# Two transformer blocks on one core: the last norm on VectorE with a store per chunk, half of each boundary's sum ahead of the last square, and weight blocks of the heads split in four parts

## The chip, the core and the metric

The kernel runs on one NeuronCore of a Trainium2 chip. The metric is the device time of one execution in microseconds. In the text PE is TensorE, DVE is VectorE, ACT is ScalarE, POOL is GpSimd and SP is SyncE, which here only issues transfers. L661 is line 661 of the kernel before.

## What is computed

The reference chains two models, each of two layers, over 512 tokens of width 1024, all in fp32. The first has attention with 12 heads in each layer (8 of kind A, over latents, and 4 of kind B, differential), gates, and a convolutional feed-forward part, over 512 tokens and, in its first layer, 256 context tokens beside them. The second has a pooling and gating mixer in layer 0, a sparse attention and retention mixer in layer 1, and a SwiGLU part after each. The parts of it that the change touches are the norms between stages and the end:

```python
def rms_norm(x, g):
    xf = x.astype(jnp.float32)
    y = xf * lax.rsqrt(jnp.mean(xf * xf, axis=-1, keepdims=True) + EPS)
    return (y * g.astype(jnp.float32)).astype(x.dtype)

    for layer in range(DEPTH):          # the second model
        h = rms_norm_2(x, ln_mix_pre[layer])
        m = even_mixer(h, ...) if layer % 2 == 0 else odd_mixer(h, ...)
        x = x + rms_norm_2(m, ln_mix_post[layer])
        h = rms_norm_2(x, ln_ffn_pre[layer])
        x = x + rms_norm_2(swiglu(h, ...), ln_ffn_post[layer])
    return x
```

## The kernel before

Activations lie transposed in SBUF: 8 chunks (DC) of 128 channels by 512 tokens. Every fp32 product is made of three matmuls of split operands (high by high, high by low, low by high; mm3, L661 to L663, and the same for several outputs at once, mm3_side, L676 to L678). Each engine has a program of its own in a fixed order written out by hand; they meet at semaphores only, so an engine that waits holds up all that stands behind it in its program.

**Weights.** The weights are cut into blocks of mostly 128 x 2048 words, in the order of split_order(). SP loads a block into one of two raw slots. ACT copies it with rounding into the high half of one of two split slots (act_prepare, L621), which must be free: the product that used it two blocks ago must have ended. DVE subtracts to get the low half (dve_prepare, L632), after which PE may use the block (pe_block) and SP may load the next into the raw slot. One block is one ACT instruction and one DVE instruction, put by hand between other work.

**Heads.** head_items() makes one list of steps for a layer's 12 heads, and PE, ACT and DVE each walk it, each doing its own share of a step: projections of queries and keys (a_q, a_k, v_b, b_qk, b_rope), early gates, scores (PE L1264, maximum on DVE L1587, exp on ACT L1410, division on DVE "weigh" L1492 to L1502), "turn" (PE transposes L1296, ACT L1420, DVE L1595) and "values". A turn is one chunk of 256 keys of one pair of query tiles; each turn holds at most a few pieces of the next head's projections. 13 blocks are prepared in each layer's list, each at the point where the product that held its slot has just ended.

**Boundaries.** Between stages a norm needs the sum over all 1024 channels of the squares. ACT squares a chunk (L692, chunk 0 in L705), POOL adds chunks 1 to 6 to chunk 0 (L715), and PE sums over the channels with a matrix of ones: pe_square_summed, L718, one fp32 matmul for POOL's sum (L722) and one for the square of chunk 7 (L723), each recorded as two. ACT then makes the logarithm (L728) and the root (L733). After the out projection (act_out_linear) a chunk is first copied out of PSUM (act_evict, L2174) and then squared. DVE applies the norm, adds to x and makes the low half of the next input chunk by chunk (dve_post_gained: L2124, L2128, L2088), while ACT makes the high halves (act_gained_highs, L2073). At the end of act_out_linear, and of act_glu and dve_glu in layer 0, one block is prepared between the last square and the logarithm, on ACT and on DVE.

**End.** After the last feed-forward part DVE multiplies the eight chunks (dve_post_norm, L2117), POOL adds each to x (pool_post_norm, L2137), and one transfer of 2048 KB stores all (L3536).

## Time and profile before

| | us |
|---|---|
| median of 3 runs | 3604.68 (3600.24 to 3604.97) |
| the profiled execution | 3599.33, of it the span 3597.3 |
| PE busy | 3355.3 (93%) |
| DVE busy | 1954.5 (54%) |
| ACT busy | 1394.8 (39%) |
| POOL busy | 334.0 (9%) |
| DMA | 321.93 MB, mean 89 GB/s |

The span runs from the first to the last instruction of the core. PE's matmuls overlap each other and their ends are modelled, so its busy share says where it works, not how well. The trace lists every instruction with its start and length, and, in brackets, how long its engine had been idle and which instruction ended that. A mean granted clock of 1.0 is TensorE's full 2.4 GHz.

### The profile page before, as it was taken

What the parts mean: (1) busy time and instruction counts of PE and PEld (TensorE: products, weight loads), DVE (VectorE), ACT (ScalarE), POOL (GpSimd) and SP (SyncE); (2) the same over time, 40 slices, a digit from 0 to 9 for tenths busy, and PEclk for the clock granted to TensorE, in tenths of its full rate; (3) what the DMA queues carried; (4) which work ended last, traced back from release to release, by engine and by line L of the source; (5) the groups of instructions that cost most, each with busy time, mean ns of one, the idle gap of its engine ahead of it and who ended that gap; (6) DMA issues with size and microseconds to landing.
All of it is one profiled execution on the core that took longest, in us unless ns stands there. A gap on an engine that the chain in (4) does not pass through costs nothing.

```text
span 3597.3 us, 41937 instructions
## 1 busy us (share of the span) xinstructions
PE 3355.3 (93%) x17348; PEld 2804.3 (78%) x17348; DVE 1954.5 (54%) x2794; ACT 1394.8 (39%) x2200; POOL 334.0 (9%) x277
## 2 busy tenths in 40 slices
PE   8889898999999997898899999899999989989997
PEld 5778777888888886787777888787888767768886
DVE  5674555677736635756535635455444566345243
ACT  4563443234313324644434323344222356243221
POOL 0010000221101110000011101121000210210002
PEclk9999999999999999999899999999999999999999
DMA  5001114343323422011133332322222310122322
GB/s 224 32 26 50 50 39 163 133 145 123 113 83 127 137 76 70 19 63 46 59 132 123 128 106 87 101 94 85 90 104 88 108 37 35 59 70 87 107 87 72
DMA packets 74495, 321.93 MB, mean 89 GB/s; under 512 B 8897, under 2 KB 17857, under 8 KB 52289
## 3 DMA queue, kind: packets, MB, share of 16 engines
q1 hardware_dynamic: 74304, 319.25, 25.9%
q8 instruction: 137, 2.24, 0.3%
q14 instruction: 54, 0.43, 0.0%
HBM read 303.49 MB, written 15.73 MB: 89 GB/s over the span
## 4 chain that ended last, share of the span: by engine, by line
PE 49%; DVE 5%; ACT 3%; issue 1%; POOL 0%; DMA 0%; POOLq 0%; DVEq 0%; ACTq 0%; SPq 0%
PE psum L661 14%; PE psum L663 14%; PE psum L662 14%; PE psum L1264 1%; ACT split_weights L621 1%; DVE split_weights L632 1%; PE psum L1296 1%; ACT arena L1410 0%; PE psum L2560 0%; DVE arena L2124 0%; PE psum L676 0%; DVE arena L1587 0%; PE psum L2975 0%; PE psum L677 0%; PE psum L678 0%
## 5 line engine op out<-in xcount | busy, mean ns | idle before, releaser
L661 PE MATMUL psum<-split_inputs,split_weights 128*128 128x512 f32 (+1 forms) x2864 | 1055.0, 368 | 19.5 <-DVE split_weights L632 14.0
L662 PE MATMUL psum<-split_inputs,split_weights 128*128 128x512 f32 (+1 forms) x2864 | 1046.2, 365 | 0.0
L663 PE MATMUL psum<-split_inputs,split_weights 128*128 128x512 f32 (+1 forms) x2864 | 1045.4, 365 | 0.0
L632 DVE TENSOR_TENSOR split_weights<-arena,split_weights 128x2048 fp32r<-128x2048 f32 (+3 forms) x246 | 506.2, 2058 | 483.5 <-ACT split_weights L621 483.1
L661 PEld LDWEIGHTS psum<-split_inputs,split_weights 128*128 128x128 f32 x2864 | 544.1, 190 | 113.0 <-DVE split_weights L632 17.2
L662 PEld LDWEIGHTS psum<-split_inputs,split_weights 128*128 128x128 f32 x2864 | 543.9, 190 | 87.9 <-issue 2.8
L663 PEld LDWEIGHTS psum<-split_inputs,split_weights 128*128 128x128 f32 x2864 | 543.0, 190 | 87.9
L621 ACT ACTIVATE split_weights<-arena 128x2048 fp32r<-128x2048 f32 (+3 forms) x246 | 414.0, 1683 | 162.2 <-PE psum L663 162.1
L661 PE MATMUL psum<-split_hidden,split_weights 128*128 128x512 f32 (+1 forms) x880 | 324.1, 368 | 2.4 <-DVE split_weights L632 2.4
L662 PE MATMUL psum<-split_hidden,split_weights 128*128 128x512 f32 (+1 forms) x880 | 323.9, 368 | 0.0
L663 PE MATMUL psum<-split_hidden,split_weights 128*128 128x512 f32 (+1 forms) x880 | 323.7, 368 | 0.0
L715 POOL TENSOR_TENSOR arena<-arena 128x512 f32<-128x512 f32 x84 | 107.0, 1278 | 1025.2 <-ACT arena L692 1023.0
L661 PEld LDWEIGHTS psum<-split_hidden,split_weights 128*128 128x128 f32 x880 | 165.9, 189 | 31.1 <-DVE split_weights L632 3.5
L663 PEld LDWEIGHTS psum<-split_hidden,split_weights 128*128 128x128 f32 x880 | 165.9, 189 | 27.7
L662 PEld LDWEIGHTS psum<-split_hidden,split_weights 128*128 128x128 f32 x880 | 165.9, 189 | 27.2
L1264 PE MATMUL psum<-split_high 128*128 128x512 f32 (+3 forms) x864 | 154.1, 362 | 35.0 <-ACT arena L1410 26.9
L1640 DVE CUSTOM_DVE_ANT_0 arena<-arena 128x1024 f32<-128x1024 f32 x128 | 164.8, 1287 | 27.8 <-DMA arena<-w_ada_dram 24.3
L1587 DVE TENSOR_REDUCE arena<-psum 128x1 f32<-128x768 f32 (+1 forms) x160 | 132.3, 845 | 86.4 <-PE psum L1264 85.6
L692 ACT ACTIVATE arena<-arena 128x512 f32<-128x512 f32 (+1 forms) x131 | 75.7, 588 | 260.5 <-DVE arena L1969 98.1
L1264 PEld LDWEIGHTS psum<-split_high 128*128 128x128 f32 (+1 forms) x864 | 121.0, 199 | 68.4 <-ACT arena L1410 35.5
L1410 ACT ACTIVATE arena<-psum,arena 128x768 f32<-128x768 f32 (+1 forms) x160 | 129.6, 813 | 51.0 <-DVE arena L1587 50.5
L1979 POOL TENSOR_TENSOR arena<-arena 128x512 f32<-128x512 f32 x66 | 72.9, 1105 | 726.0 <-DVE arena L1946 726.0
(353 smaller groups left out, 4784.6 us busy)
## 6 DMA issues: line engine op xcount, KB each, us to landing
arena<-w_up_dram SPq DMA_DIRECT2D x44, 1024.0 KB, 5.9
arena<-ffn_up_dram SPq DMA_DIRECT2D x44, 1024.0 KB, 4.8
arena<-w_ada_dram SPq DMA_DIRECT2D x80, 512.0 KB, 3.8
arena<-w_in_dram SPq DMA_DIRECT2D x32, 1024.0 KB, 4.9
arena<-w_down_dram SPq DMA_DIRECT2D x32, 704.0 KB, 4.2
arena<-ffn_down_dram SPq DMA_DIRECT2D x32, 704.0 KB, 4.1
arena<-od_w_in_dram SPq DMA_DIRECT2D x13, 1024.0 KB, 4.8
arena<-w_ada_dram SPq DMA_DIRECT2D x8, 1024.0 KB, 12.6
```

Of the source, the lines that this page charges most:

```text
L621: act.e.activation(ws[:, i % N_SLOTS, 0, 0:nk * w], raw_view(key), ACT.Copy).then_inc(*w_hi(*key))
L632: dve.e.tensor_tensor(ws[:, i, 1, 0:nk * w], raw_view(key), ws[:, i, 0, 0:nk * w].bitcast(F32), ALU.subtract).then_inc(*w_lo(*key))
L661: pe.e.matmul(dst, a[0], b[0], start=i == 0, stop=False)
L662: pe.e.matmul(dst, a[0], b[1], start=False, stop=False)
L663: ins = pe.e.matmul(dst, a[1], b[0], start=False, stop=i == n - 1)
L692: act.e.activation(row, view, ACT.Square, **more).then_inc(*squared(site, s, c))
L715: pool.e.tensor_tensor(acc, acc, rows.at(site, s, c)[:, 0:w], ALU.add).then_inc(*rows.back((site, s, c), pooled, site, s, c))
L1264: return pe.e.matmul(psum[:, at_bank + x:at_bank + y], a, b, start=i == 0, stop=i == 2)
L1410: act.e.activation(row[:, 0:p["keys"]], psum[:, b:b + p["keys"]], ACT.Exp, bias=st[:, sub:sub + 1], accum_out=st[:, 2 + sub:3 + sub]).then ...
L1587: dve.e.tensor_reduce(st[:, sub:sub + 1], psum[:, b:b + p["keys"]], AX.X, ALU.max, negate=True).then_inc(*maxed(l, t, sub))
L1640: dve.e.tensor_tensor_reduce(part.get("junk", rstd_all), ADA[slots[n % len(slots)]], wide[:, s, :], 1.0, 0.0, ALU.mult, ALU.add, mods[al][ ...
L1979: pool.e.tensor_tensor(ya, ya, yb, ALU.mult).then_inc(*added("up", l, half, m, s))
```

## The change

It has five parts.

1. pe_square_summed waits for the last square after the matmul of POOL's sum and not ahead of it.
2. In act_out_linear chunk 7 is squared straight from PSUM and copied out after that.
3. The block that was prepared between the last square and the logarithm moves: ACT makes its high half in two halves behind the high halves of chunks 2 and 4 (act_gained_highs), DVE its low half at the end of dve_post_gained, ahead of the block that was there already. This holds for three boundaries: behind each out projection and behind layer 0's feed-forward part.
4. The last norm and its addition are both on DVE, chunk by chunk one behind the other, and SP stores each chunk of 256 KB when it is done.
5. In the heads each prepare becomes four of a quarter. They queue up in a list, preps; at the end of a turn's pieces at most two are put out, and the rest is put out ahead of a step that takes a new block (v_b, b_qk of queries, the first gate of a chunk). The wait for the slot and the raw block stands ahead of each; PE waits for the last quarter only.

```diff
--- before.py
+++ after.py
@@ -308,6 +308,9 @@
             "ffn": halves(layer, 20, 24, 2) + halves(layer + 1, 0, 8, 2) + halves(layer + 1, 8, 20, 1)}[stage]
 
 
+PARTS = 4
+
+
 def head_items(layer, engine):
 
 
@@ -372,7 +375,7 @@
         out += [("late",) + x for x in step if x[0] in ("a_q", "a_k")]
     out += start
     out += [("weigh", t) for _, t in start]
-    late, weigh, values, ob = [], [], [], {}
+    late, weigh, values, ob, preps = [], [], [], {}, []
 
     def of_values(x, i, c):
 
@@ -405,15 +408,25 @@
             out += scores[0:1]
         weigh = [t for _, t in scores]
         of_norm(x, "ob_root")
-        out += gates[x]
+        if gates[x] and gates[x][0][2:] == (LAT, 0):
+            out += preps
+            preps = []
+        out += [y for y in gates[x] if y[0] != "prepare"]
+        preps += [("prepare", part, PARTS) for y in gates[x] if y[0] == "prepare" for part in range(PARTS)]
         late += [("gate_out",) + y[1:] for y in gates[x] if y[0] == "gate"]
         for step in plan[x]["pieces"]:
-            out += step
+            if step[0][0] == "v_b" or step[0][0] == "b_qk" and step[0][3:] == (0, LAT):
+                out += preps
+                preps = []
+            out += [y for y in step if y[0] != "prepare"]
             late += [("late",) + y for y in step if y[0] in ("a_q", "a_k")]
+            preps += [("prepare", part, PARTS) for y in step if y[0] == "prepare" for part in range(PARTS)]
+        for _ in range(min(len(preps), 2)):
+            out.append(preps.pop(0))
         out += scores[1:]
         of_norm(x, "ob_norm")
         of_norm(x, "ob_square")
-    out += late
+    out += late + preps
     for x, y in enumerate(values, len(slots)):
         of_values(x, *y)
         of_norm(x, "ob_square")
@@ -608,30 +621,44 @@
             _, nk, w = block_shape(*key)
             return raw[raw_slot(key)][:, 0:nk * w]
 
-        def act_prepare():
+        def part_of(part, n):
+
+            return slice(0, n) if part is None else slice(part[0] * n // part[1], (part[0] + 1) * n // part[1])
+
+        def act_prepare(part=None):
+
             if act_next[0] == len(blocks):
                 return
             key = blocks[act_next[0]]
-            act_next[0] += 1
+            last = part is None or part[0] == part[1] - 1
+            act_next[0] += last
             _, nk, w = block_shape(*key)
-            i = block_no[key]
+            i, cols = block_no[key], part_of(part, nk * w)
             if i >= N_SLOTS and book:
                 act.wait_ge(product, *book["ended"][blocks[i - N_SLOTS]])
             act.wait_ge(raw_in[raw_slot(key)], *key)
-            act.e.activation(ws[:, i % N_SLOTS, 0, 0:nk * w], raw_view(key), ACT.Copy).then_inc(*w_hi(*key))
-
-        def dve_prepare():
+            act.e.activation(ws[:, i % N_SLOTS, 0, cols], raw_view(key)[:, cols], ACT.Copy).then_inc(
+                *(w_hi(*key) if last else w_hi(*key, part[0])))
+
+        def dve_prepare(part=None):
+
             if dve_next[0] == len(blocks):
                 return
             key = blocks[dve_next[0]]
-            dve_next[0] += 1
-            use(key)
+            last = part is None or part[0] == part[1] - 1
+            dve_next[0] += last
+            if part is None or part[0] == 0:
+                use(key)
             _, nk, w = block_shape(*key)
-            i = block_no[key] % N_SLOTS
-            dve.wait_ge(w_hi, *key)
-            dve.e.tensor_tensor(ws[:, i, 1, 0:nk * w], raw_view(key), ws[:, i, 0, 0:nk * w].bitcast(F32),
-                                ALU.subtract).then_inc(*w_lo(*key))
-            free(key)
+            i, cols = block_no[key] % N_SLOTS, part_of(part, nk * w)
+            if last:
+                dve.wait_ge(w_hi, *key)
+            else:
+                dve.wait_ge(w_hi, *key, part[0])
+            ins = dve.e.tensor_tensor(ws[:, i, 1, cols], raw_view(key)[:, cols], ws[:, i, 0, cols].bitcast(F32), ALU.subtract)
+            if last:
+                ins.then_inc(*w_lo(*key))
+                free(key)
 
         def pe_block(*key):
             pe.wait_ge(w_lo, *key)
@@ -717,9 +744,9 @@
 
         def pe_square_summed(site, s, n, w, which):
             pe.wait_ge(pooled, site, s, n - 2)
-            pe.wait_ge(squared, site, s, n - 1)
             ps = banks.take(pe, site, s, place=6 + which)
             pe.e.matmul(ps[:, 0:w], ones, rstd[:, which, 0:w], start=True, stop=False)
+            pe.wait_ge(squared, site, s, n - 1)
             pe.e.matmul(ps[:, 0:w], ones, rows.at(site, s, n - 1)[:, 0:w], start=False, stop=True).then_inc(
                 *rows.back((site, s, n - 1), product, "square", site, s, n - 1))
 
@@ -1353,7 +1380,7 @@
             for item in head_items(l, "act"):
                 what, at = item[0], item[1:]
                 if what == "prepare":
-                    act_prepare()
+                    act_prepare(at)
                 elif what == "a_q":
                     n, h, s = at
                     hi = q_half(n, 0)[:, s[0]:s[1]]
@@ -1506,7 +1533,7 @@
             for item in head_items(l, "dve"):
                 what, at = item[0], item[1:]
                 if what == "prepare":
-                    dve_prepare()
+                    dve_prepare(at)
                 elif what == "a_q":
                     n, h, s = at
                     if s == LAT:
@@ -2072,6 +2099,8 @@
                 act.wait_ge(halves_sum, y_site, c)
                 act.e.activation(h2_part(c, *ALL)[0], X2[:, c, :], ACT.Copy, scale=v2(l, gname, c)).then_inc(
                     *h_hi(site, c))
+                if c in (2, 4):
+                    act_prepare((c // 2 - 1, 2))
             for c in range(DC):
                 act_square_summed(site, ALL, c, DC, T2, 1, X2[:, c, :])
 
@@ -2113,9 +2142,14 @@
 
         def dve_post_norm(site, l, gname):
             dve.wait_ge(rooted, site, ALL)
-            for c in range(DC):
-                dve.e.scalar_tensor_tensor(out=MX[:, c, :], in0=MX[:, c, :], scalar=v2(l, gname, c), in1=rstd[:, 0, :],
-                                           op0=ALU.mult, op1=ALU.mult).then_inc(*normed(site, c))
+            for c in range(DC + 1):
+                if c < DC:
+                    dve.e.scalar_tensor_tensor(out=MX[:, c, :], in0=MX[:, c, :], scalar=v2(l, gname, c),
+                                               in1=rstd[:, 0, :], op0=ALU.mult, op1=ALU.mult).then_inc(*normed(site, c))
+                if c:
+                    dve.wait_ge(normed, site, c - 1)
+                    dve.e.tensor_tensor(X2[:, c - 1, :], X2[:, c - 1, :], MX[:, c - 1, :], ALU.add).then_inc(
+                        *conv("final", c - 1))
 
         def dve_post_gained(site, l, gname, then, then_l, then_gname):
             dve.wait_ge(rooted, site, ALL)
@@ -2130,11 +2164,7 @@
                 if c > 1:
                     dve_gained(then, v2(then_l, then_gname, c - 2), c - 2)
             dve_prepare()
-
-        def pool_post_norm(site):
-            for c in range(DC):
-                pool.wait_ge(normed, site, c)
-                pool.e.tensor_tensor(X2[:, c, :], X2[:, c, :], MX[:, c, :], ALU.add).then_inc(*added(site, c))
+            dve_prepare()
 
 
         HS_REST = hs[:, 2 * DC * T2:2 * DC * N_TOK].rearrange("p (s c t) -> p s c t", s=2, c=GC)
@@ -2190,10 +2220,14 @@
             for m in range(DC):
                 if m % 2 == 0:
                     act_prepare()
+                if m == DC - 1:
+                    act.wait_ge(product, name, m)
+                    act_square_summed(site, ALL, m, DC, T2, 0, banks.at(name, m))
+                    act_evict((name, m), MX[:, m, :])
+                    continue
                 act_evict((name, m), MX[:, m, :])
                 act.wait_ge(copied, name, m)
                 act_square_summed(site, ALL, m, DC, T2, 0, MX[:, m, :])
-            act_prepare()
             act_log(site, ALL, DC, T2, 0, D)
             act_root(site, ALL, T2, 0)
 
@@ -2391,8 +2425,6 @@
                 act_prepare()
                 act.wait_ge(conv, "glu_down", l, c)
                 act_square_summed(("ffn", l), ALL, c, DC, T2, 0, MX[:, c, :])
-            if l == 0:
-                act_prepare()
             act_log(("ffn", l), ALL, DC, T2, 0, D)
             act_root(("ffn", l), ALL, T2, 0)
 
@@ -2427,8 +2459,6 @@
                 dve.wait_ge(copied, "glu_down", l, 0, c)
                 dve.e.tensor_tensor(MX[:, c, :], MX[:, c, :], banks.at("glu_down", l, 1, c), ALU.add).then_inc(
                     *banks.back(("glu_down", l, 1, c), conv, "glu_down", l, c))
-            if l == 0:
-                dve_prepare()
 
 
         BIG = 1.5 * 2.0 ** 23
@@ -3318,7 +3348,7 @@
                     dve.e.tensor_tensor(lo, OY[:, h, :], hi.bitcast(F32), ALU.subtract).then_inc(*h_lo("od_y", ALL, h))
 
         def dve_out_linear():
-            for _ in range(DC // 2 + 1):
+            for _ in range(DC // 2):
                 dve_prepare()
 
 
@@ -3526,15 +3556,15 @@
                 if l == 0:
                     for c in range(DC):
                         pool_square_summed("mix_1", ALL, c, DC, T2, 1)
-            pool_post_norm(("ffn", 1))
 
         def sync_program():
             sp_setup()
             for what in errands:
                 sp_errand(*what)
-            sp.wait_ge(added, ("ffn", DEPTH - 1), DC - 1)
-            sp.e.dma_start(out.rearrange("(c p) t -> p c t", p=P), X2).then_inc(*stored())
-            sp.wait_ge(stored)
+            for c in range(DC):
+                sp.wait_ge(conv, "final", c)
+                sp.e.dma_start(out[c * P:(c + 1) * P, :], X2[:, c, :]).then_inc(*stored(c))
+            sp.wait_ge(stored, DC - 1)
 
         block = ctx.enter_context(nc.Block())
```

## Rows read from the trace of the kernel before

**Rows 1.** Page: the header.
```profile
span 3597.3 us, 41937 instructions
```
**Rows 2.** PE's waits over the whole span: us in total, times, longest.
```profile
PE psum L722 <- issue: 5.9, 4, 1.6
...
PE psum L722 <- ACT arena L692: 3.0, 2, 1.6
```
**Rows 3.** Timeline of PE at the end: start, length, line, shape, count, idle.
```profile
3573.72 1.10 PE L722 MATMUL psum<-arena 128*128 128x512 f32 x2 [1.49 <-issue]
3574.66 1.02 PE L723 MATMUL psum<-arena 128*128 128x512 f32 x2
```
**Rows 4.** Timeline of ACT at the boundary behind layer 0's out projection.
```profile
2445.13 0.60 ACT L2174 ACTIVATE arena<-psum 128x512 f32<-128x512 f32 x1 [4.17 <-PE psum L663]
2445.76 0.63 ACT L692 ACTIVATE arena<-arena 128x512 f32<-128x512 f32 x1
...
2448.48 0.69 ACT L728 ACTIVATE arena<-psum,arena 128x512 f32<-128x512 f32 x1 [0.29 <-PE psum L723]
```
**Rows 5.** Timeline of DVE at the same boundary.
```profile
2448.22 2.29 DVE L632 TENSOR_TENSOR split_weights<-arena,split_weights 128x2048 fp32r<-128x2048 f32 x1 [8.58 <-ACT split_weights L621]
2450.43 1.41 DVE L2124 SCALAR_TENSOR_TENSOR arena<-arena 128x512 f32<-128x512 f32 x2
2451.76 0.68 DVE L2128 TENSOR_TENSOR arena<-arena 128x512 f32<-128x512 f32 x1
2452.36 0.75 DVE L2124 SCALAR_TENSOR_TENSOR arena<-arena 128x512 f32<-128x512 f32 x1
...
2464.53 1.63 DVE L2088 SCALAR_TENSOR_TENSOR split_inputs<-arena,split_inputs 128x512 fp32r<-128x512 f32 x2
```
**Rows 6.** Timeline of PE at the same boundary: the next block's first matmul.
```profile
2468.31 0.39 PE L661 MATMUL psum<-split_inputs,split_weights 128*128 128x512 f32 x1
```
**Rows 7.** Timelines of DVE, POOL and SP at the end.
```profile
3577.10 10.40 DVE L2117 SCALAR_TENSOR_TENSOR arena<-arena 128x512 f32<-128x512 f32 x8 [4.14 <-ACT arena L733]
...
3577.93 11.57 POOL L2137 TENSOR_TENSOR arena<-arena 128x512 f32<-128x512 f32 x8 [10.41 <-DVE arena L2117]
...
3589.52 0.39 SPq L3536 DMA_DIRECT2D out_dram<-arena  x1
```
**Rows 8.** Page: a DMA issue, with count, KB each, us to landing.
```profile
g_store<-arena SPq DMA_DIRECT2D x16, 256.0 KB, 2.0
```
**Rows 9.** PE's waits in the heads of layer 0, 116 to 616 us.
```profile
PE psum L1296 <- DVE arena L1494: 11.8, 7, 5.2
...
PE psum L1264 <- DVE split_high L1595: 5.4, 1, 5.4
PE psum L1296 <- DVE arena L1502: 4.3, 2, 4.2
...
PE psum L1243 <- DVE split_high L1595: 3.1, 1, 3.1
```
**Rows 10.** PE's waits in the heads of layer 1, 1416 to 1826 us.
```profile
PE psum L1264 <- ACT arena L1410: 15.0, 6, 3.6
```
**Rows 11.** Timelines of ACT and DVE in layer 1's heads, around one prepared block.
```profile
1736.62 1.91 ACT L621 ACTIVATE split_weights<-arena 128x2048 fp32r<-128x2048 f32 x1
...
1738.56 2.29 DVE L632 TENSOR_TENSOR split_weights<-arena,split_weights 128x2048 fp32r<-128x2048 f32 x1 [1.38 <-ACT split_weights L621]
1740.77 1.82 DVE L1587 TENSOR_REDUCE arena<-psum 128x1 f32<-128x768 f32 x2
```
**Rows 12.** Timeline of PE in layer 1's heads.
```profile
1726.09 0.47 PE L661 MATMUL psum<-split_inputs,split_weights 128*128 128x512 f32 x1 [2.11 <-DVE split_high L1595]
...
1736.23 1.43 PE L1264 MATMUL psum<-split_high 64*128 64x512 f32 x12
...
1742.80 2.68 PE L1264 MATMUL psum<-split_high 64*128 64x512 f32 x12 [3.37 <-ACT arena L1410]
```
**Rows 13.** One stretch of layer 1's heads: busy us of each engine, then PEclk.
```profile
1740.00:1800.00 60.00, 49.58 (x258) 40.38 (x258) 37.01 (x56) 28.13 (x54) 0.00 (x0) 0.86 0.19 62
```

## Prediction, made before the changed kernel was run

> **What bounds the kernel now.** First the page: the span is 3597.3 us [rows 1] and PE is the busiest engine by far, so time can only be won where PE stands still, where it runs at a lower clock, or at the end, where it is done. The second view is the list of PE's waits. It shows three kinds of places. At six boundaries PE waits 1.4 to 1.6 us for the last square and then makes both halves of the sum [rows 2]. In the heads it waits for DVE and ACT, up to 5.4 us at a time [rows 9, 10], and the timeline of the third view shows a prepared block just ahead of the long ones [rows 11, 12]. And behind the last matmul nothing runs beside the chain: sum, root, DVE, POOL, store [rows 3, 7]. Elsewhere PE has its weights in time.
>
> The profiled execution took 3599.33 us, 2.03 beyond its span. I sum against its own time; the median of the runs shown is 5.35 above it, and I take the same gap for the changed kernel.
>
> **1. Half of the sum ahead of the last square.** At the end the first half of the sum starts at 3573.72 after 1.49 us of waiting, the second at 3574.66 [rows 3]. The first half so costs 0.94 us, and it fits in the wait: POOL's sum that it needs is a whole chunk of matmuls older. The second half then starts when the square is there, at 3573.72. That is 0.94 us for each of the six boundaries where PE waits (the 4 and 2 waits of [rows 2]): layer 1's out projection and the double boundary of the first model, two out projections and two feed-forward ends of the second. The other places where the sum is made have no such wait (PE has other matmuls to do), and there I take nothing: the same two matmuls in the same order.
>
> **2. The last square straight from PSUM.** At the out projection of the second model the copy starts at 2445.13, the square at 2445.76, the logarithm, which waits for the second half, at 2448.48 [rows 4]; the second half takes 1.02 [rows 3], so it started at 2447.43. Afterwards the square starts at 2445.13 and is there at about 2445.8; the first half of the sum, 0.94 from the product's end at 2445.1, ends at 2446.05, so now the sum itself is late, and the second half starts then: 1.38 us earlier, part 1 included. The copy, 0.60 us, lies beside the second half. This holds twice.
>
> **3. The block moved off the boundary.** At the end, where no block is in the way, DVE starts 3577.10 - 3574.66 = 2.44 us after the second half of the sum [rows 3, 7]. Here that would be 2449.87, but DVE still has its block till 2450.51 and starts at 2450.43 [rows 5]: the block costs 0.56 us already, and would cost all that parts 1 and 2 win if it stayed. Without it DVE starts at 2446.05 + 2.44 = 2448.49, 1.94 us earlier. Behind layer 0's feed-forward part, which looks the same but for part 2, it is 0.94 + 0.56 = 1.5 us. What is late next: DVE works at three instructions a chunk, two of 0.66 and one of 0.60 from start to start, 1.92 us, and ACT has one high half of about 0.7 in that time; half a block is about 1.0 us of ACT (half of 1.91 and some [rows 11]) and just fits behind chunks 2 and 4. On DVE the block now stands behind the last low half, 2.29 us [rows 5], while PE still has its last chunk to do: from the last low half, ended at 2466.16, to the next block's first matmul at 2468.31 were 2.15 us [rows 5, 6], so PE waits 0.1 to 0.2 us for the block. Queued behind the block on DVE is only the next block, needed much later. Net: 2 x 1.8 + 1.4 + 2 x 0.94 (the two boundaries of the first model) = 6.9 us. Bounds: 5.2 if ACT's halves slip by one chunk, 7.5 if PE waits for nothing.
>
> **4. The end.** DVE and POOL together took from 3577.10 to 3589.50, then came one store; from its issue at 3589.52 to the end of the span are 7.8 us [rows 1, 7]. Eight norms took 10.40 us, 1.30 each, while POOL worked beside them; with POOL at rest the same kind takes 0.66 from start to start and an addition 0.60 [rows 5]. So DVE alone does a chunk in 1.26: first addition 1.33 after the start, the seventh at 8.9, the eighth, which has to wait for its own norm, at about 9.5, ended at 10.2. It starts 0.94 us earlier (part 1), at 3576.16, and ends at 3586.35, 3.1 us ahead of POOL. The last store is 256 KB; such stores took 2.0 us to land [rows 8], and 0.4 us of closing work as before: end at 3588.8, 8.5 us earlier, of which 0.94 is part 1. The stores before it have 1.26 us each, and 2048 KB in 7.8 us says that 256 KB move in under 1 us, so none waits for another. Bounds: 7 (the last lands after 3.5) to 9.
>
> The Trainium skill speaks against this part: "DMA: Bandwidth & Descriptors", section "Measured (HBM→SBUF, 128 partitions, SWDGE, issued from GpSimd)", wants transfers of 1 MiB or more, since small ones pay the fixed cost each time. The sum above has it paid once, behind the last chunk; paid eight times in a row it is the third rival below. By the fit on that page of the Trainium skill (about 2.0 us plus bytes over 436 GB/s, an estimate of 2.6 us for 256 KB) the end would come 0.6 us later than by the row; no row here shows a run of small stores.
>
> **5. Quarters in the heads.** The terms are in one example [rows 11, 12]. ACT starts the block at 1736.62, DVE waits for it, subtracts 2.29 us, and only at 1740.77 takes the maximum of scores whose matmuls had started at 1736.23 and took 1.43. Then comes exp, then PE, which stood still for 3.37 us, and does in 2.68 us 12 matmuls of the kind that took 1.43 before the wait: the granted clock of this stretch is 0.86 [rows 13], so part of it ran at 1.2 GHz instead of 2.4.
> With two quarters DVE waits 0.63 (ACT's time for 512 columns [rows 4]) and subtracts twice, 0.60 from start to start [rows 5]: 1.9 us instead of 4.15, so DVE goes on 2.25 us earlier. Four in a row, where a step takes a new block, hold it for 3.1. All four cost ACT about 2.2 instead of 1.9 and DVE 2.4 instead of 2.2; over 26 blocks that is 5 to 8 us of either, which is lost only where that engine is the late one.
> What it gives, wait by wait:
> - layer 1, three waits of about 3.4 before double scores (most of the 15.0 us in [rows 10]): 2.2 each, 6.7.
> - layer 0: of the 5.4 before L1264, where the rope steps now also come first, 1.8; of the 4.2 before L1296, 1.9; of the 5.2 before L1296 only 0.7, since there DVE is the late engine and gets the other two quarters one turn on; of the 3.1 before L1243 and its twin on the other buffer, 0.9 each, since a block that used to lie in an idle stretch of DVE now lies closer to them [rows 9]. Together 6.2.
> - some nine waits of 1.5 to 2.5 us that follow a block in either layer, about half a microsecond each where ACT or DVE comes out of the block sooner, 5 in all (an estimate from the 2.25 above, a quarter of it each).
> - the clock: behind each of the three large waits up to 1.7 us of slow matmuls; the waits left are about 1.1. I take 3 of 5.
> - against it a new wait. The second two quarters come one turn later, and PE may be there first. I find it at two gates of layer 1. At one, PE's first gate matmul at 1726.09 already waited 2.11 us [rows 12]; the block's last quarter would be ready at about 1725.5, so of these 2.1 only 0.6 go (counted among the small ones). At the gate before it PE would wait about 1.3.
> - and the other two quarters of some 20 blocks hold DVE a second time, 1.2 to 1.9 us, mostly while PE is in 24 or 48 matmuls of a projection (5 to 11 us of cover). If a fifth of them isn't covered, 4 lost.
> 6.7 + 6.2 + 5 + 3 - 1.3 - 4 = 15.6 us, say 16. Bounds: 0 (every second pair is late) to 28 (all clock, nothing lost).
>
> A second rule of the Trainium skill, "VectorE: DVE Perf Modes", section "The TRN2 errata — SBUF-src ops pay a fixed extra latency per instruction", says that each instruction with operands in SBUF pays a fixed latency, so splitting costs. By that fit of the Trainium skill four quarters would take 2.76 us, 0.47 more than one of 2.29; back to back the row has 0.60 from start to start, 2.4 in all. By the Trainium skill's figure the quarters would give 2 or 3 us less.
>
> **Sum.** 6.9 + 8.5 + 16 = 31.4. 3599.33 - 31.4 = 3567.9; with the 5.35 to the median 3573.3, say 3573.
>
> **Rivals.**
> - The gain in the heads fades: the wait only moves a turn, because DVE has as much to do as before. DVE is busy 62% of [rows 13], PE 83%, which speaks against it; that the 5.2 us wait sits in a stretch where DVE is late speaks for it. Then only 15.4 are won: 3589. Chance 0.2.
> - The clock comes back too: the short waits no longer bring TensorE down, and most of the 5 us and those in layer 0 are won, with no new waits: 31.4 + 13 = 44: 3560. Chance 0.15.
> - The stores pay in turn, each 2.0 us [rows 8] behind the one before: from the first addition's end at 3578.2 the last lands at 3594.2 and the span ends at 3594.6, 2.7 instead of 8.5 won: 3579. The rows speak for overlap only by the rate of one large store. Chance 0.07. (The rule of the Trainium skill above would point this way.)
> - Slower than before: the second pair of quarters holds DVE 1.9 us at each of some 20 turns with no cover, and PE's gates wait for the last quarter. 20 x 1.9 = 38 lost, the first pairs win nothing against it, and with 15.4 won it is 22.6 slower: 3627. It decides if DVE has less than 1.9 us idle in those turns. In [rows 13], where parts of three blocks fall, it is idle 23 of 60 us. Chance 0.03.
> - The change doesn't do what it says in part 1: POOL's sum comes as late as the square, and PE waits as before. 6 us fewer, 3579. A chunk of matmuls lies between the two; chance 0.02.
>
> **How the numbers follow.** My case has 0.53: 3573, by itself 3563 to 3583. The range of 8 in 10 takes in the rival without the heads and most of the one with the clock: 3558 to 3591. About 0.2%, 7 us, is what a measurement of this kernel can tell. Only the slower rival, or an unseen wait in the heads that eats 8 of the 15.4, is not faster: faster 0.92, same 0.05, slower 0.03.
>
> **What would show it.** At the six boundaries L722 starts with no wait behind the last product and L723 within 1.0 us (0.1 behind out projections); DVE's first norm about 2448.5 less what was won before; at the end eight stores 1.26 us apart and 2.4 us from the last addition to the end. In the heads the L1264 waits of layer 1 shrink from 3.4 to about 1.1, 12 matmuls take near 1.43, and a wait of L661 for L632 appears at the gates of layer 1. If the page shows PE's waits in the heads unchanged in sum but on other lines, part 5 was wrong; if DVE's norms at the end take more than 0.66, part 4.

## The result, and the profile of the changed kernel

The changed kernel takes 3557.28 us (median of 4 runs, 3556.24 to 3559.71) against 3602.46 of the kernel before in the same job (3598.44 to 3604.97): ratio 0.9874, 95% interval 0.9858 to 0.9890, 45.2 us faster. Forecast were 3573 with a range of 3558 to 3591, so the time lies 0.7 us below the range. The profiled execution took 3556.24 us.

Where the 42.8 us between the two spans (3597.3 and 3554.5) come from, cut at the first matmul of scores and at the last of values that reads split_high alone in each layer (six matmuls and one last wait come behind it, 1.6 us before and 0.7 now in layer 0):

| stretch | before, us | changed, us | won | forecast |
|---|---|---|---|---|
| start | 128.2 | 129.3 | -1.1 | 0 |
| heads of layer 0 | 441.5 | 431.6 | 9.9 | heads together 16 |
| between the heads | 866.8 | 866.7 | 0.1 | 0 |
| heads of layer 1 | 362.0 | 342.8 | 19.2 | |
| rest | 1798.8 | 1784.1 | 14.7 | 15.4 |

The rest came as forecast, the heads gave 29.1 us, nearly twice the 16.

PE's waits over the whole span (us, times, longest). L688 is L661 of before, L658 is L632, L1291 is L1264, L1437 is L1410:

```profile
span 3554.5 us, 42096 instructions
...
PE psum L688 <- DVE split_weights L658: 29.6, 16, 4.6
PE psum L1291 <- ACT arena L1437: 19.4, 18, 2.0
...
PE psum L750 <- ACT arena L719: 2.5, 4, 0.6
```

The waits ahead of the sum's second half are what is left of [rows 2]: at most 0.6 us each. In the heads of layer 1 (window 1416 to 1826 before, 1405 to 1800 here), and below that those of layer 0:

```profile
PE psum L688 <- DVE split_weights L658: 9.2, 5, 2.5
PE psum L1291 <- ACT arena L1437: 6.7, 6, 1.3
...
PE psum L1291 <- ACT arena L1437: 12.8, 12, 2.0
PE psum L1323 <- DVE arena L1521: 9.2, 7, 2.9
...
PE psum L1291 <- DVE split_high L1622: 2.9, 1, 2.9
PE psum L1323 <- DVE arena L1529: 2.4, 2, 2.2
...
PE psum L1270 <- DVE split_high L1622: 1.8, 1, 1.8
```

Against [rows 9, 10]: the wait for exp in layer 1 fell from 15.0 to 6.7 (longest 3.6 to 1.3), and the new wait for the low half came, 9.2 in 5 instead of 3.7 in 2. Of these 9.2, 5.4 lie in the heads, in three waits (2.5, 0.8 and 2.1), the last of them in place of the 2.11 us of [rows 12]. The turn that [rows 11, 12] showed looks so now (ACT, DVE, PE):

```profile
1718.23 1.14 ACT L640 ACTIVATE split_weights<-arena 128x512 fp32r<-128x512 f32 x2
...
1721.09 0.90 ACT L1437 ACTIVATE arena<-psum,arena 128x768 f32<-128x768 f32 x1 [0.59 <-DVE arena L1614]
...
1722.01 0.90 ACT L1437 ACTIVATE arena<-psum,arena 128x768 f32<-128x768 f32 x1
...
1718.89 1.29 DVE L658 TENSOR_TENSOR split_weights<-arena,split_weights 128x512 fp32r<-128x512 f32 x2
1720.10 1.82 DVE L1614 TENSOR_REDUCE arena<-psum 128x1 f32<-128x768 f32 x2
...
1717.85 1.43 PE L1291 MATMUL psum<-split_high 64*128 64x512 f32 x12
...
1722.13 2.24 PE L1291 MATMUL psum<-split_high 64*128 64x512 f32 x12 [1.09 <-ACT arena L1437]
```

From ACT's first quarter (1718.23) to the maximum (1720.10) are 1.87 us; forecast were 1.9, before it was 4.15. PE waits 1.09 instead of 3.37.

The boundary behind layer 0's out projection (PE, DVE, PE) and the end (DVE, SP):

```profile
2415.92 1.02 PE L748 MATMUL psum<-arena 128*128 128x512 f32 x2
2416.78 1.12 PE L750 MATMUL psum<-arena 128*128 128x512 f32 x2
...
2419.32 1.41 DVE L2158 SCALAR_TENSOR_TENSOR arena<-arena 128x512 f32<-128x512 f32 x2 [8.69 <-ACT arena L760]
...
2437.30 0.50 PE L688 MATMUL psum<-split_inputs,split_weights 128*128 128x512 f32 x1
```

```profile
3539.24 1.13 PE L750 MATMUL psum<-arena 128*128 128x512 f32 x2 [0.58 <-ACT arena L719]
...
3541.79 1.42 DVE L2147 SCALAR_TENSOR_TENSOR arena<-arena 128x512 f32<-128x512 f32 x2 [3.26 <-ACT arena L760]
...
3550.71 1.29 DVE L2151 TENSOR_TENSOR arena<-arena 128x512 f32<-128x512 f32 x2
...
3543.83 8.52 SPq L3566 DMA_DIRECT2D out_dram<-arena  x8
```

The second half starts 0.86 us behind the first and DVE 2.54 behind that, so no block is in the way. At the end the last addition is done at 3552.00 and the span ends 2.5 us later; DVE alone does a chunk in 1.26 to 1.27 us.

### The profile page after: what moved, and what is told of

Same layout as the page of the kernel before. It is cut to its first block, busy times and chain, and to the rows that moved or that the text cites. A ratio compares the mean times of both kernels' runs of the same rounds, so it can differ in the third digit from the quotient of the medians.

```text
span 3554.5 us, 42096 instructions
## 1 busy us (share of the span) xinstructions
PE 3348.7 (94%) x17348; PEld 2799.1 (79%) x17348; DVE 1958.8 (55%) x2880; ACT 1402.4 (39%) x2281; POOL 324.9 (9%) x269
## 3 DMA queue, kind: packets, MB, share of 16 engines
q8 instruction: 137, 2.24, 0.3%
## 4 chain that ended last, share of the span: by engine, by line
PE 50%; DVE 5%; ACT 3%; issue 1%; POOL 0%; DMA 0%; DVEq 0%; ACTq 0%; POOLq 0%; SPq 0%
PE psum L688 14%; PE psum L689 14%; PE psum L690 14%; PE psum L1291 1%; DVE split_weights L658 1%; PE psum L1323 1%; ACT split_weights L640 1%; DVE arena L2158 0%; ACT arena L1437 0%; PE psum L703 0%; PE psum L3005 0%; PE psum L704 0%; PE psum L705 0%; PE psum L2590 0%; PE psum L3029 0%
## 5 line engine op out<-in xcount | busy, mean ns | idle before, releaser
L688 PE MATMUL psum<-split_inputs,split_weights 128*128 128x512 f32 (+1 forms) x2864 | 1053.8, 368 | 20.4 <-DVE split_weights L658 17.3
L658 DVE TENSOR_TENSOR split_weights<-arena,split_weights 128x2048 fp32r<-128x2048 f32 (+6 forms) x324 | 513.2, 1599 | 423.2 <-ACT split_weights L640 422.0
L688 PEld LDWEIGHTS psum<-split_inputs,split_weights 128*128 128x128 f32 x2864 | 543.3, 190 | 114.8 <-DVE split_weights L658 21.9
L640 ACT ACTIVATE split_weights<-arena 128x2048 fp32r<-128x2048 f32 (+6 forms) x327 | 423.9, 1314 | 163.7 <-PE psum L690 163.6
L688 PE MATMUL psum<-split_hidden,split_weights 128*128 128x512 f32 (+1 forms) x880 | 324.3, 368 | 2.4 <-DVE split_weights L658 2.4
L688 PEld LDWEIGHTS psum<-split_hidden,split_weights 128*128 128x128 f32 x880 | 166.0, 189 | 31.1 <-DVE split_weights L658 3.5
L1291 PE MATMUL psum<-split_high 128*128 128x512 f32 (+3 forms) x864 | 150.1, 353 | 24.6 <-ACT arena L1437 19.4
L1291 PEld LDWEIGHTS psum<-split_high 128*128 128x128 f32 (+1 forms) x864 | 118.0, 193 | 57.0 <-ACT arena L1437 27.8
L1437 ACT ACTIVATE arena<-psum,arena 128x768 f32<-128x768 f32 (+1 forms) x160 | 129.6, 812 | 40.4 <-DVE arena L1614 39.7
```

Of the source, the lines that this page charges most:

```text
L640: act.e.activation(ws[:, i % N_SLOTS, 0, cols], raw_view(key)[:, cols], ACT.Copy).then_inc(*(w_hi(*key) if last else w_hi(*key, part[0])))
L658: ins = dve.e.tensor_tensor(ws[:, i, 1, cols], raw_view(key)[:, cols], ws[:, i, 0, cols].bitcast(F32), ALU.subtract)
L688: pe.e.matmul(dst, a[0], b[0], start=i == 0, stop=False)
L1291: return pe.e.matmul(psum[:, at_bank + x:at_bank + y], a, b, start=i == 0, stop=i == 2)
L1437: act.e.activation(row[:, 0:p["keys"]], psum[:, b:b + p["keys"]], ACT.Exp, bias=st[:, sub:sub + 1], accum_out=st[:, 2 + sub:3 + sub]).then ...
```

## Experiments

In every trace I read three things in each layer's heads, between the same two matmuls as above: the time, the sum of PE's waits in the view of waits, and what the clock took, the sum over windows of 10 us of (1 - granted clock) x length. "Filling" stands for matmuls whose result nobody reads, ahead of a wait. Each row is one trace.

| kernel | heads 0, heads 1, us | PE waits | clock |
|---|---|---|---|
| before | 441.5, 362.0 | 46.8, 40.6 | 23.8, 17.2 |
| changed | 431.6, 342.8 | 39.8, 31.2 | 18.7, 5.1 |
| part 5 alone | 429.8, 342.3 | 39.2, 31.0 | 18.8, 5.1 |
| parts 1 to 4 | 442.1, 362.9 | 46.4, 39.7 | 25.5, 18.9 |
| whole blocks, new places | 446.5, 360.1 | 50.1, 41.8 | 25.5, 15.3 |
| four quarters, old places | 432.7, 346.0 | 40.4, 32.2 | 20.4, 8.6 |
| four quarters, new places | 441.8, 349.2 | 45.3, 33.8 | 23.9, 10.2 |
| halves, one a turn | 432.4, 348.2 | 40.5, 33.4 | 20.6, 8.5 |
| before, layer 1 filled | 442.3, 353.0 | 46.4, 31.7 | 25.7, 5.1 |
| before, layer 0 filled | 435.3, 363.1 | 39.2, 39.8 | 17.1, 18.9 |
| changed, nine waits filled | 424.2, 342.0 | 32.8, 26.4 | 10.2, 3.4 |
| the same, and three boundaries filled | 427.0, 342.0 | 32.5, 26.4 | 13.7, 3.4 |
| exp three times | 431.5, 352.4 | 39.9, 35.8 | 18.8, 11.9 |
| exp three times, filled | 429.9, 346.6 | 39.8, 27.6 | 17.1, 3.4 |

**Part 5 alone, and parts 1 to 4 alone.** The first is the kernel before with the diff's parts of head_items, act_prepare and dve_prepare, the second the rest of the diff.

> Only part 5 (quarters in the heads), everything else as before. Theory A (my reading after the result: the trace of the changed kernel is about 28 us ahead behind both heads lists, 9 in layer 0 and 18 to 19 in layer 1, against 16 forecast; the rest is as forecast): 27 to 28 us faster than before, near 3575. Theory B (the forecast's sizes, and the surplus is something that only the whole change gives): 16 us, near 3586. Under A the slow stretches of TensorE in the heads go with it: granted clock of 1740 to 1800 us up from 0.86.

> Parts 1 to 4 alone, blocks of the heads whole and in the old place. The forecast had 6.9 + 8.5 = 15.4 us faster than before, near 3587; and if the parts add up, it and the kernel with part 5 alone sum to 45 us.

Part 5: 0.9907 (0.9894 to 0.9921), 33 us. Parts 1 to 4: 0.9966 (0.9954 to 0.9979), 12 us. They add up to the 45 of the whole. Theory A holds: the granted clock of 1740 to 1800 us is 0.94 with part 5 alone. Part 5 was sized much too small. Parts 1 to 4 were forecast at 15.4; the boundaries and the end, read one by one below, add up to 14.8 us. The median shows 3 less. In the trace of parts 1 to 4 both heads and the mixer of layer 1, which these parts leave alone, took 2.1 us more together than before; the rest isn't explained.

**Cutting or moving.** Three kernels take the two apart:

```diff
-PARTS = 4
+PARTS = 1
```

> The changed kernel with blocks in one piece (PARTS = 1): each block is put out where the list puts its first quarters, at the end of the turn's pieces, but whole. Tells moving from splitting. Theory A (splitting does it, a turn carries half a block instead of one): the waits of 3.4 us before the scores of layer 1 come back, and the kernel is 15 to 25 us slower than the changed one, 3572 to 3582. Theory C (the place does it, since the rope steps and gates now stand ahead of the block): within 5 us of the changed one.

```diff
-        out += [y for y in gates[x] if y[0] != "prepare"]
-        preps += [("prepare", part, PARTS) for y in gates[x] if y[0] == "prepare" for part in range(PARTS)]
+        out += in_parts(gates[x])
...
-            out += [y for y in step if y[0] != "prepare"]
+            out += in_parts(step)
...
-        for _ in range(min(len(preps), 2)):
-            out.append(preps.pop(0))
```

(in_parts replaces a prepare by its four quarters.)

> The changed kernel with the four quarters back to back at the old place of the block. Tells the pipelining of ACT and DVE inside a block (DVE starts after a quarter, not after a whole block) from the spreading over two turns. By the forecast four in a row hold DVE for 3.1 us instead of 4.15, 1.05 of the 2.25 us: then about half of the gain in the heads stays, 12 to 16 of 28 us, total near 3570. If the spreading is all of it, near 3585. If the overlap is all of it, near 3557.

```diff
-        for _ in range(min(len(preps), 2)):
+        for _ in range(len(preps)):
```

> The changed kernel with all four quarters put out at the end of the same turn's pieces: the places of the kernel with whole blocks moved, the cut of the changed one. That one took 446.5 and 360.1 us in the two heads, the one with quarters in the old place 432.7 and 346.0. If cutting alone does it wherever the block stands, 432 to 436 and 343 to 347, near 3560. If the new place is bad and only the spreading makes up for it, 440 and 353 or more, near 3575.

Whole blocks in the new places: 0.9968 (0.9956 to 0.9980), which is the gain of parts 1 to 4 alone: at 3590 us it missed both expectations on the slow side, since whole blocks lose more in layer 0 at the new place than at the old. Four quarters in the old places: 0.9902 (0.9889 to 0.9916), 3568 us; the total came as expected, but of the gain in the heads 24.8 us of 29.1 stayed and not half. Four in the new: 0.9917 (0.9904 to 0.9931), 3576 us; the heads took 441.8 instead of 432 to 436 us and 349.2 instead of 343 to 347, so the place matters too. The table reads as a square. At the old places cutting wins 8.8 us in layer 0 and 16.0 in layer 1. The new places are worth -5.0 and +1.9 to a whole block, and are 9.1 and 3.2 us worse than the old for four quarters. Two turns instead of one win 10.2 and 6.4 from there. So the cut does most of it; the two turns mostly pay for the new place, and only 1.1 and 3.2 us are on top of quarters left where the block was; 1.1 is less than traces of the same heads differ by.

Why quarters in the old place did so well, the turn of [rows 11, 12] shows only in part (ACT, DVE, PE):

```profile
1716.24 2.18 ACT L635 ACTIVATE split_weights<-arena 128x512 fp32r<-128x512 f32 x4
...
1719.31 1.82 DVE L1609 TENSOR_REDUCE arena<-psum 128x1 f32<-128x768 f32 x2
...
1721.34 3.21 PE L1286 MATMUL psum<-split_high 64*128 64x512 f32 x12 [2.29 <-ACT arena L1432]
```

From ACT's start to the maximum are 3.07 us, as counted (3.1), and PE waits 2.29 instead of 3.37. The three large waits of layer 1 fell by only 1.0 to 1.1 us each; the rest of the 16.0 lies in other waits (all together 8.4 less) and in the clock, which took 8.6 less.

**Halves.**

> The changed kernel with two halves for each block of the heads and one half a turn: the same words per turn as two quarters. If it is the size of the lump that a turn carries that counts, within 3 us of the changed kernel (a half holds DVE 1.0 + 1.2 = 2.2 us instead of 1.9 for two quarters; both together 3.3 instead of 3.1): heads 431 to 434 us in layer 0 and 342 to 346 in layer 1, between first scores and last values, near 3559. If fine steps between ACT and DVE are what counts, 5 us or more slower than the changed kernel.

0.9880 (0.9867 to 0.9894): 3562 us, which the intervals can't tell from the changed kernel. Layer 0 is like it; layer 1 took 348.2 where 342 to 346 were expected, with 2.2 us more of waits and 3.4 of slow clock. That lies between the two readings, so whether fine steps count is open.

**The clock, with the waits left as they are.** Ahead of three waits for exp in layer 1 PE makes 14 matmuls into the PSUM bank whose turn is next:

```diff
+                    def fill_wait(n, q0):
...
+                        pe.e.matmul(banks.views[place][:, 0:N_LAT], q_half(n, 0)[:, q0:q0 + P], k_half(n, 0)[:, 0:N_LAT],
+                                    start=True, stop=True)
...
+                    for _ in range(14 if l == 1 and t in (35, 39, 43) else 0):
+                        fill_wait(n, q0)
                     half_banks(0)
```

> The kernel before; ahead of its three long waits in layer 1's heads (3.61, 3.37 and 3.37 us for ACT's exp) PE makes 14 matmuls of 128x512 into a free PSUM bank, about 3.1 us, whose result nobody reads. The wait itself and everything on ACT and DVE stay. Theory A (the clock falls because PE stands still): the 12 score matmuls behind go from 3.10, 3.21 and 2.68 us to 1.43, 4.7 us won there and up to 8 in all, near 3595; the waits at t = 33 and 47 (1.46, 2.19), which get no such matmuls, keep their slow groups of 2.2 and 3.2. Theory B (the clock falls for another reason, so that only the shorter waits count): no gain, 3600 to 3603, and the groups stay at about 3.

> The kernel before with unused matmuls (5, 9, 9, 9) ahead of four waits for exp in layer 0's heads (1.09, 2.03, 2.03, 2.03 us), which the quarters did not shorten. The changed kernel has the same waits there and lost 5.1 us less to the clock in layer 0 than before. If these waits bring the clock down by themselves: 4 to 8 us won in layer 0 (441.5 to 434 to 437). If it is the pile of other waits around blocks that does: under 2.

Layer 1 filled: 0.9978 (0.9970 to 0.9987), 8 us, and 9.0 in the heads of layer 1 in the trace, with nothing changed on ACT and DVE. Windows of 10 us at the three waits, before and then filled; the first of each also holds the wait or its filling (length; busy us and instructions of PE, PEld, DVE, ACT, POOL; then PEclk):

```profile
1636.00:1646.00 10.00, 6.39 (x34) 5.05 (x32) 8.54 (x11) 4.48 (x9) 0.00 (x0) 0.83 0.30 107
1686.00:1696.00 10.00, 10.00 (x39) 8.16 (x39) 8.25 (x15) 4.04 (x9) 0.00 (x0) 0.66 0.31 118
1742.00:1752.00 10.00, 9.20 (x41) 7.63 (x42) 7.34 (x12) 5.05 (x11) 0.00 (x0) 0.83 0.25 76
```

```profile
1636.00:1646.00 10.00, 9.59 (x60) 7.54 (x60) 8.03 (x10) 5.22 (x8) 0.00 (x0) 1.00 0.28 107
1683.00:1693.00 10.00, 9.81 (x51) 7.66 (x50) 9.20 (x13) 5.53 (x12) 0.00 (x0) 1.00 0.68 238
1735.00:1745.00 10.00, 9.81 (x53) 7.75 (x52) 9.13 (x12) 5.75 (x12) 0.00 (x0) 1.00 0.24 79
```

The granted clock stays at its upper level, 2.4 GHz. Before, it was the lower one far behind the group: behind the second wait, which ended at 1685.79, matmuls of 128x512 took 0.63 us and only from 1693.24 on, 7.4 us later, 0.40:

```profile
1692.40 0.63 PE L661 MATMUL psum<-split_inputs,split_weights 128*128 128x512 f32 x1
...
1693.24 0.40 PE L663 MATMUL psum<-split_inputs,split_weights 128*128 128x512 f32 x1
```

The last of the three waits in PE's timeline, filled:

```profile
1735.81 3.33 PE L1261 MATMUL psum<-split_high 128*128 128x512 f32 x14
1739.34 2.24 PE L1273 MATMUL psum<-split_high 64*128 64x512 f32 x12 [0.19 <-ACT arena L1421]
```

The groups of 12 came down only to 2.24, not to 1.43 as I expected: a group that starts when its first bank is free waits inside for the second exp, which in the turn shown above starts 0.92 us behind the first. So of the 3.10, 3.21 and 2.68 us before only 0.86, 0.97 and 0.44 were slow clock, 2.3 in all; the other 6.7 us were lost behind the groups, in matmuls that the forecast didn't look at. Not all of them lie close to the three waits. Laid side by side, the two traces differ by 1.3, 2.9 and 1.5 us up to the next scores behind each, 5.8 in all; 1.6 more lie behind the wait of 2.11 us at 1726.09 and 1.6 behind the last wait for exp, neither of which had filling. Where slow stretches fall changes from trace to trace: in the two others with the same heads in layer 1 (parts 1 to 4, and layer 0 filled) the three waits by themselves cost 9.1 and 9.3 us more than the filled ones. So filling is worth 9 us or a little more in this layer, and a single wait has no fixed price.

Layer 0 filled ahead of four waits: 0.9975 (0.9966 to 0.9984), 9 us, and 6.2 us in its heads, with waits of 1.1 and 2.0 us only, inside the 4 to 8 expected.

**The clock, the other way round.** In the changed kernel ACT makes the exp of three tiles three times over, which brings the long waits back without a block:

```diff
+                        for j in range(2 if l == 1 and t in (34, 38, 42) and sub == 0 else 0):
+                            act.e.activation(row[:, 0:p["keys"]], psum[:, b:b + p["keys"]], ACT.Exp, bias=st[:, sub:sub + 1]
+                                             ).then_inc(*again(t, j))
+                            act.wait_ge(again, t, j)
```

> The changed kernel; at three places of layer 1's heads (the tiles ahead of the waits that were 3.61, 3.37, 3.37 us before and are 1.33, 1.09, 1.09 now) ACT makes the same exp three times over instead of once, so PE's waits are back at about 3.1 to 3.4 us while the blocks stay in quarters. Two exps are about 1.9 us. Theory A (half or more of what such a wait costs is the clock behind it): the heads of layer 1 take 342.8 + 3 x 1.9 + up to 9 of slow clock = 355 to 358 us, and the clock loss there goes from 5 back to 12 to 17. Theory B (a wait costs its length): 348.5, clock loss 5.

> The same with 13 matmuls of 128x512 (2.8 us), whose result nobody reads, ahead of the three long waits. ACT and DVE are as late as in the kernel with exp three times. Theory A: the clock stays up, so 348 to 350 us in the heads of layer 1, clock loss 5, and 6 to 9 us faster than without these matmuls. Theory B: no difference between the two.

0.9901 (0.9887 to 0.9916) without filling, 0.9867 (0.9852 to 0.9882) with it. The third of the waits, PE's timeline and then the window behind it, without filling:

```profile
1731.04 2.50 PE L1292 MATMUL psum<-split_high 64*128 64x512 f32 x12 [2.96 <-ACT arena L1442]
```

```profile
1731.00:1741.00 10.00, 9.96 (x45) 8.29 (x46) 6.06 (x10) 5.18 (x11) 0.00 (x0) 0.83 0.17 54
```

and with it (13 matmuls):

```profile
1718.71 3.11 PE L1289 MATMUL psum<-split_high 128*128 128x512 f32 x13
1721.83 2.19 PE L1301 MATMUL psum<-split_high 64*128 64x512 f32 x12
```

```profile
1718.00:1728.00 10.00, 9.99 (x54) 7.91 (x53) 8.36 (x15) 8.47 (x16) 0.00 (x0) 1.00 0.16 52
```

The heads of layer 1 took 9.6 us more, less than the 12 to 15 expected, and with filling 3.8 more, less than the 5 to 7 expected. At the three waits themselves it is 7.9 and 3.4 us; the rest lies behind other waits. PE's three waits grew by 5.6 us in all, so theory B, that a wait costs its length, falls: 7.9 is more and 3.4 is less. Filling took away 4.6 of the 7.9. That the clock adds only 2.3 to the length is in part because there were slow matmuls behind the first of the three in the changed kernel already (12 in 2.81 us, where 2.24 is the time at full clock).

**Filling as a means.** The changed kernel with 4 to 9 such matmuls ahead of nine waits for exp, first together with 22 matmuls behind the sum at three boundaries, then alone:

> The changed kernel with such matmuls (4 to 9 each) ahead of nine waits for exp in both heads, and 22 matmuls of ones by ones behind the sum at three boundaries of the second model, where PE waits 5.5 us for the first low half. Results unused. Under theory A the groups of 12 behind the nine waits fall from 2.2 to 3.3 us to 1.43: 10.5 us. At the boundaries DVE's chunk (1.92 us) is slower than PE's six matmuls at full clock (1.3) and faster than at half (2.6), so a clock kept up gives 1 to 2 us each, 4 in all. Together 14, near 3543. Under theory B nothing, near 3557, or a few us more where a filler outlasts its wait.

> The changed kernel with the unused matmuls ahead of nine waits for exp in the heads only, blocks outside the heads whole. Tells which of its two edits made the fastest kernel (3546, against 3557) fast. If the clock: 5 to 9 us faster than the changed kernel, 3548 to 3552. If the halves outside the heads, which alone gave 0 to 4: 3555 to 3557.

Both places: 0.9856 (0.9840 to 0.9873), 3552 us where 3543 was expected. Heads alone: 0.9838 (0.9825 to 0.9852), 3544.39 us, 13 us below the changed kernel and the fastest that I ran. In its trace the heads are 8.2 us shorter, inside the expected 5 to 9; the rest lies in stretches that filling doesn't touch. With the same heads the trace with both places won 5.4 there, and its mixer of layer 1 took 3.6 us longer, so the 7 us between the two kernels are no sign that filling at the boundaries costs. At the boundaries filling won nothing: 32.44 us from the sum behind the out projection to the next, 32.40 without. It does keep the clock, though. The first is 4 us of the changed kernel, some 7 us behind the sum's second half, the others a window as far behind it in the filled kernel and the start of a chunk there:

```profile
2424.00:2428.00 4.00, 4.00 (x11) 3.13 (x10) 4.00 (x7) 2.40 (x3) 0.00 (x0) 0.50 0.02 4
```

```profile
2420.00:2424.00 4.00, 3.51 (x14) 2.27 (x13) 4.00 (x8) 2.40 (x3) 0.00 (x0) 1.00 0.00 0
```

```profile
2425.36 0.50 PE L703 MATMUL psum<-split_inputs,split_weights 128*128 128x512 f32 x1 [0.28 <-DVE split_inputs L2136]
```

DVE is busy all the time in either: it needs 1.93 us a chunk, and PE, which at half clock falls behind (2.56 us for its six matmuls), has caught up by the last chunk. So a slow clock cost nothing here, where DVE is the late engine.

**Part 3 and part 4 undone.** The block back between the last square and the logarithm (and out of act_gained_highs); and one store behind the last addition:

```diff
                 act_square_summed(site, ALL, m, DC, T2, 0, MX[:, m, :])
+            act_prepare()
             act_log(site, ALL, DC, T2, 0, D)
```

(One of its places; the same is put back behind layer 0's feed-forward part and on DVE.)

> The changed kernel with part 3 undone: the block is again prepared between the last square and the logarithm, on ACT and DVE, at three boundaries. The forecast: DVE's first norm then waits for the block (low half ends 5.4 us behind the start of the last copy, as before), so all that parts 1 and 2 win there is lost but the clock: 5.0 to 5.3 us slower than the changed kernel, near 3562. If the block isn't in the way (the rival that the square was the only late thing): 0 to 2 us slower.

> The changed kernel, but with the one store of 2048 KB behind the last addition instead of eight of 256 KB. Norm and addition stay on DVE. Before, from the store's issue to the span's end were 7.8 us; now 2.5 from the last addition. So 5.3 us slower than the changed kernel, near 3562; if small stores pay in turn as the third rival had it, the difference would be near 0.

Block back: 0.9893 (0.9880 to 0.9907). By their ratios both kernels are 7 to 8 us above the changed one, where 5 was expected. Within one trace the stretches are clearer: from one sum to the next it takes 34.04, 33.57 and 34.04 us at the three boundaries, the changed kernel 32.40, 32.41 and 32.39. That is 4.5 us, 5.0 expected. With the block,

```profile
2419.54 2.29 DVE L658 TENSOR_TENSOR split_weights<-arena,split_weights 128x2048 fp32r<-128x2048 f32 x1 [8.40 <-ACT split_weights L640]
2421.75 1.41 DVE L2156 SCALAR_TENSOR_TENSOR arena<-arena 128x512 f32<-128x512 f32 x2
```

DVE starts 4.46 us behind the sum's second half (2417.29) and not 2.54. One store: 0.9896 (0.9880 to 0.9911). It is issued at 3548.13 and the span ends at 3555.9, 7.8 us later, where eight stores end 2.5 us behind the last addition: 5.3 us, as expected.

**Halves outside the heads.**

```diff
+            if part is None and act_next[0] >= FIRST_SPLIT:
+                for p in range(2):
+                    act_prepare((p, 2))
+                return
```

(FIRST_SPLIT is 0; the same in dve_prepare.)

> The changed kernel with every block outside the heads in two halves back to back, on ACT and DVE. From ACT's start to the low half a block takes 1.9 + 2.3 = 4.2 us, in halves about 1.0 + 2.4 = 3.4. PE waits 16 times for such a low half (29.6 us in all): if each gets 0.5 to 0.8 shorter, 6 to 10 us are won, less 2 to 4 where ACT or DVE is late and pays the extra instructions: 2 to 8 us faster than the changed kernel, 3550 to 3555. If the extra instructions weigh more, slower by up to 5.

> The changed kernel with the halves outside the heads and with the unused matmuls ahead of the nine waits for exp in the heads (4.6 us in layer 0 and 0.8 in layer 1 in the kernel with both fillings), none at the boundaries, where they gave nothing (32.43 us between the sums with them, 32.40 without). The two add: 5.4 and 2 to 8, near 3546, in any case under 3557.

Alone 0.9862 (0.9849 to 0.9875), which can't be told from the changed kernel; with filling in the heads 0.9840 (0.9826 to 0.9853), the same as filling alone. Both lie where they were expected (3550 to 3555, and 3546), but that filling alone gives as much as both speaks against the reason. The halves give nothing that can be told: PE's waits for a low half grew from 29.6 to 34.8 us, and from one sum to the next 33.56 us pass instead of 32.40. There the low half takes 3.45 us instead of 2.29 (DVE, POOL, PE):

```profile
2431.86 3.45 DVE L667 TENSOR_TENSOR split_weights<-arena,split_weights 128x1024 fp32r<-128x1024 f32 x2
...
2432.28 9.92 POOL L751 TENSOR_TENSOR arena<-arena 128x512 f32<-128x512 f32 x6 [22.07 <-ACT arena L728]
...
2435.36 0.50 PE L697 MATMUL psum<-split_inputs,split_weights 128*128 128x512 f32 x1 [1.12 <-DVE split_weights L667]
```

Of POOL's additions (line L751 by itself: shortest, median and longest in ns):

```profile
L751 POOL TENSOR_TENSOR arena<-arena x6: 1287/1296/2093, 2432.3 to 2440.9; 128x512 f32<-128x512 f32 x6
```

DVE's first half took 1.22 us, the second 2.32; POOL's first two additions took 1.95 and 2.09 us, the others 1.29 or 1.30. It reads as if they took turns: POOL's first addition, started in DVE's first half, waits for its end, then DVE's second half waits for POOL, and POOL's second addition for that. The whole block held POOL off: in the changed kernel POOL's first addition there starts 0.42 us into the block and takes 3.02 us. No run took POOL's additions away from this place, so it stays a reading.

## Why the prediction was wrong, point by point

**Part 1.** Right. From the sum in the feed-forward part to the sum at its end it took 340.77 us and takes 339.79, 0.98 less (forecast 0.94). At the double boundary of the first model 371.30 + 1.72 became 370.37 + 1.82, 0.8. At the other one of the first model the second half starts 1.66 us behind the last product instead of 2.53, 0.9.

**Part 2.** Right. Up to the sum behind layer 0's out projection it took 131.2 or 132.7 us in the kernels without parts 1 and 2, and takes 129.6 or 131.1 with them, 1.6 either way, where 1.38 was forecast. What makes the two values isn't shown: with the parts the longer one goes with 1.7 us more of slow clock, without them the clock is the same.

**Part 3.** Right. The block cost 1.65, 1.16 and 1.65 us at its boundaries. With 0.2 behind each sum the out projection's boundary wins 1.8, as forecast, and the one behind layer 0's feed-forward part 1.2 (forecast 1.4). PE hardly waited for the moved block: its first matmul started 0.36 us behind the start of the one before, where 0.23 is usual.

**Part 4.** Right. From the second half of the last sum to the end of the span it was 22.6 us and is 15.3: 7.3 won, 7.6 forecast. The rival that small stores pay in turn fell: the last of eight was done 2.5 us behind the last addition, and one store takes 5.3 us more. The prediction took a rule of the Trainium skill for its rival ("DMA: Bandwidth & Descriptors", section "Measured (HBM→SBUF, 128 partitions, SWDGE, issued from GpSimd)"): at least 1 MiB for at least 75% of the peak rate. The runs here don't speak against it, since it is about a transfer's rate; what counts at the end is when the last store can start.

**Part 5, the lengths of waits.** About right. DVE's pause is 1.87 us (1.9), the three largest waits for exp in layer 1 fell by 6.8 (6.7 forecast; all six by 8.3), the wait before L1296 for L1502 by 1.9 (1.9), the twin waits of L1243 by 1.3 each (0.9). The 5.2 before L1296 fell by 2.3 and not by 0.7. The 5.4 before L1264 became 2.9 for DVE and, in the middle of the same scores, 1.8 for exp; up to the next scores 1.4 us are won there (1.8 forecast). The new waits for low halves in layer 1 are 3.3 us (1.3 + 4 forecast); the 2.11 at 1726.09 is now 2.06 for the block's last quarter and not 1.5. The second pair of quarters found its cover, so the slower rival had nothing to stand on. One step was wrong on the way: four quarters back to back were to give half of the gain and gave 8.8 and 16.0 us of 9.9 and 19.2. In the turn shown the cut is worth the 1.05 us that were counted; that it wins elsewhere too, in other waits and in the clock, was not. In sum PE's waits in the heads shrank by 7.0 and 9.4 us, 16.4, where the forecast had 12.6. And the sentence that PE has its weights in time outside the heads misread the page: PE waited 23.6 us in 12 waits for low halves before, most of it outside. The change leaves those waits, so it cost the forecast nothing.

**Part 5, the clock: the step that failed.** The prediction says "behind each of the three large waits up to 1.7 us of slow matmuls" and "I take 3 of 5". It read the slow clock from the group of 12 alone, and even that wrongly, since 0.8 of each 1.7 was the wait inside the group; what the clock takes behind the group, and behind smaller waits, was put at nothing. The heads are 29.1 us shorter and the waits in them 16.4, so 12.7 us were won in matmuls that ran faster (9.8 in layer 1 and 2.9 in layer 0; the clock column fell by 12.1 and 5.1), where the sum had 3. That is 9.7 of the 13.5 us that were missing against the 15.6 of the sum; the waits are 3.8. Filling shows the same without touching a wait: 9.0 us in layer 1 of the kernel before.

The rival "the clock comes back too" had 0.15 and gave 44 us in all, 3560. It names the right term and its number came near, in part by luck: it had no new waits and took it that short waits no longer bring TensorE down, and neither is so, since the new waits in layer 1 are 3.3 us, and filling the short waits of the changed kernel won 4.6 to 9.3 us more in layer 0 (three kernels). How much of layer 0's share belongs to which wait is open.

## What to carry to other kernels

Read the matmuls behind a wait of PE until they are fast again (here 7 us behind one wait), not only in the next group; three waits made 1.9 us longer cost 7.9 us with PE idle and 3.4 with PE kept busy, and filling a wait is a cheap test and was a gain where PE was the late engine. A long helper instruction between two engines is best cut first (quarters in the old place gave most of it) and moved second. Beside POOL's additions a cut lost: 33.56 us from sum to sum instead of 32.40.
